# Router and step-size products with stationary weights in four column quarters

## What is computed

```
# each of three expert stages (wg: 1024x4, we: 1024x16)
gl = t @ wg + bg                      # group logits
el = t @ we + be                      # expert logits, 4 groups of 4
... one group, two experts of it per token, their weights; then
... the chosen experts' gate, up and down products
# state-space block (second stack, inside h @ w_in, width 24)
dt    = softplus(dt_raw + dt_bias)    # 16 columns: step sizes
log_f = log_sigmoid(f_raw + forget_b) # 8 columns: forget gates
```

## Time and profile before

| | |
|---|---|
| median of three runs | 1569.85 us (1568.22 to 1571.46) |
| profiled execution | 1570.28 us, span from first to last instruction 1568.5 us |
| mean granted TensorE clock | 0.94 of 2.4 GHz |
| TensorE products busy | 1376.5 us, 88% |
| VectorE, ScalarE, GpSimd busy | 434.8, 238.8, 81.1 us |
| DMA | 357.54 MB, mean 228 GB/s |

### The profile page before, as it was taken

The page is one execution under the profiler, slowest core; times in us unless marked ns, Lnnn a source line. Parts: engine busy times, 40 slices in busy tenths (PEclk is TensorE's granted clock), DMA queues, the critical chain, the costliest instruction groups (busy, mean ns, idle before and its releaser), DMA issues.

```text
span 1568.5 us, 20749 instructions
## 1 busy us (share of the span) xinstructions
PE 1376.5 (88%) x8735; PEld 805.9 (51%) x8735; DVE 434.8 (28%) x1239; ACT 238.8 (15%) x591; POOL 81.1 (5%) x190
## 2 busy tenths in 40 slices
PE   3999889998997788989997999889988899757895
PEld 3446454443445555544446855554555456434574
DVE  1005452222103464432215452421125410001013
ACT  0004210101102353100012121002311120100000
POOL 1110000000010000000001000000000011101010
PEclk9999889999999599899997999899998899998998
DMA  9958627999743365359997333383366389999990
GB/s 324 358 153 293 218 106 267 353 345 324 270 161 109 106 213 165 121 186 365 346 349 255 130 138 108 108 295 107 114 217 206 107 272 333 341 327 294 309 297 28
DMA packets 264103, 357.54 MB, mean 228 GB/s; under 512 B 16086, under 2 KB 184463, under 8 KB 264011
## 3 DMA queue, kind: packets, MB, share of 16 engines
q1 hardware_dynamic: 234082, 335.72, 63.1%
q10 hardware_dynamic: 29929, 20.49, 4.6%
HBM read 355.14 MB, written 1.05 MB: 227 GB/s over the span
## 4 chain that ended last, share of the span: by engine, by line
PE 74%; DMA 12%; DVE 8%; issue 2%; ACT 2%; SPq 1%; POOL 0%; DVEq 0%; ACTq 0%; POOLq 0%
PE bank L1942 18%; PE bank L2104 7%; DMA ring<-in_w_up 5%; PE bank L2130 4%; PE bank L2145 4%; PE bank L2545 4%; PE bank L2162 4%; PE bank L2300 4%; PE bank L2032 4%; DMA ring<-in_w_down 3%; PE bank L1957 3%; PE bank L2592 3%; DMA ring<-in_w_gate 2%; PE bank L2365 2%; PE bank L2270 2%
## 5 line engine op out<-in xcount | busy, mean ns | idle before, releaser
L1942 PE MATMUL bank<-ring,hT 128*128 128x512 f32 x416 | 182.4, 600 | 3.2 <-ACT hT L810 3.0
L1942 PEld LDWEIGHTS bank<-ring,hT 128*128 128x128 f32 x416 | 79.8, 193 | 103.2 <-issue 99.8
L2104 PE MATMUL bank<-ring,A 128*64 128x512 f32 x512 | 113.4, 595 | 6.1 <-issue 3.2
L1942 PE MATMUL bank<-ring,OT 128*128 128x512 f32 x256 | 113.5, 605 | 3.0 <-ACT OT L1096 1.3
L2300 PE MATMUL bank<-ring,A 128*64 128x256 f32 x768 | 94.5, 402 | 23.0 <-DMA ring<-in_w_up 18.0
L1957 PE MATMUL bank<-ring,cact 128*32 128x128 f32 x2304 | 82.4, 297 | 23.2 <-DMA ring<-in_ada_w 14.9
L1957 PEld LDWEIGHTS bank<-ring,cact 128*32 128x32 f32 x2304 | 68.0, 119 | 36.3 <-issue 24.6
L2300 PEld LDWEIGHTS bank<-ring,A 128*64 128x64 f32 x768 | 56.8, 145 | 56.8 <-DMA ring<-in_w_up 20.7
L1942 PEld LDWEIGHTS bank<-ring,OT 128*128 128x128 f32 x256 | 49.4, 194 | 64.7 <-issue 61.0
L2104 PEld LDWEIGHTS bank<-ring,A 128*64 128x64 f32 x512 | 36.2, 137 | 72.0 <-issue 68.7
L2130 PE MATMUL bank<-pb 128*128 128x128 f32 (+1 forms) x512 | 64.4, 279 | 7.7 <-DVE A L1390 5.4
(11 more groups left out here) (405 smaller groups left out, 1651.9 us busy)
## 6 DMA issues: line engine op xcount, KB each, us to landing
ring<-in_ada_w SPq DMA_DIRECT2D x24, 2048.0 KB, 9.0
ring<-in_moe_w_gate SPq DMA_DIRECT2D x32, 1024.0 KB, 7.2
ring<-in_moe_w_up SPq DMA_DIRECT2D x32, 1024.0 KB, 9.9
ring<-in_moe_w_down SPq DMA_DIRECT2D x16, 2048.0 KB, 13.0
ring<-in_w_gate SPq DMA_DIRECT2D x16, 2048.0 KB, 18.5
ring<-in_w_up SPq DMA_DIRECT2D x16, 2048.0 KB, 17.5
ring<-in_w_in SPq DMA_DIRECT2D x13, 2048.0 KB, 12.6
ring<-in_w_mod SPq DMA_DIRECT2D x12, 2048.0 KB, 8.2
```

Of the source, the lines that this page charges most:

```text
L1942: ins = mm(B[2 * (m % 2) + tt][:], lhs[:, c, tt * P:(tt + 1) * P], w[:, c, :], start=c == 0, stop=c == C - 1)
L2104: ins = mm(B[4][n * b:n * (b + 1), :], h3[:, c, n * b:n * (b + 1)], wv[b][:, :, c, :], start=c == 0, stop=c == C - 1)
```

## The change

The roles of the two operands are exchanged. The narrow weights (20 or 24 columns) become stationary, in column quarter q = c mod 4 of the array, and 128 tokens of `hT` move; the result has the logits in the partitions 32q up and the tokens in the free dimension, in `B[2]`, as four partial sums, each of two chunks. A zero product over all partitions starts the bank (`thin_products`). ScalarE copies the 128 x 256 result to SBUF (`thin_copied`, into `PT`), and `thin_folded` multiplies it, as stationary operand, with `fold`, four 24 x 24 identities below one another: this adds the quarters and turns the tokens back into the partitions, in the bank where VectorE expects them. In the three routers the first token tile's products stand ahead of the second tile's transposes; the step sizes' fold stands behind xbc's first tile. `fold` lies in unused columns of `cols`, and GpSimd makes it ahead of the identity. Two waits of VectorE on semaphores of their own (`comb_ready`, `moe_main`) become the general step wait.

```diff
--- before.py
+++ after.py
@@ -249,6 +249,12 @@
         return ap.unsqueeze(axis).broadcast_to(shape)
 
 
+
+
+    fold = cols[:, 320:344]
+    thin = PT[:].rearrange("p a b -> p (a b)")[:, 0:T]
+    THIN = {"h1": 0, "h3": 1, "h4": 2, "h5": 3}
+
     def trans_evacuated(eng, k):
 
         eng.wait_ge(s["tr_act"] if k % 2 == 0 else s["tr_dve"], k // 2 + 1)
@@ -630,7 +636,11 @@
             pool.wait_ge(s["pool_step"], steps[0])
 
         g = nc.gpsimd
+        g.memset(fold, 0.0)
         step(g.memset(ident[:], 0.0))
+        for q in range(4):
+            step(g.affine_select(out=fold, in_=fold, compare_op=ALU.not_equal, fill=1.0, base=-32 * q,
+                                 pattern=[[-1, 24]], channel_multiplier=1))
         step(g.affine_select(out=ident[:], in_=ident[:], compare_op=ALU.not_equal, fill=1.0, base=0,
                              pattern=[[-1, P]], channel_multiplier=1))
         g.memset(zeros[:], 0.0)
@@ -780,6 +790,11 @@
                 if k % 2 == 0:
                     act.wait_ge(s["tr_ready"], k + 1)
                     op(k - TRANS[name], B[4]).then_inc(s["tr_act"], 1)
+
+        def thin_copied(hname):
+
+            act.wait_ge(s["thin_made"], THIN[hname] + 1)
+            a.copy(thin, B[2][:, 0:T]).then_inc(s["thin_out"], 1)
 
         def mod_out(G):
 
@@ -1013,6 +1028,7 @@
         trans_out("h1", modulated(0, 3), [0])
         gate_rows(1)
         trans_out("h1", modulated(0, 3), [1])
+        thin_copied("h1")
         routing_exp(act, "moe0")
         moe_act("moe0")
         mod_out(3)
@@ -1047,10 +1063,12 @@
         act.wait_ge(s["proj_dve"], PROJ_DVE[PROJ["odout"] + 1])
         act.dma_start(rowp[:, 0, :], p["final_g"].partition_broadcast(P)).then_inc(s["rows_param"], 16)
         trans_out("h3", modulated(1, 3), [1])
+        thin_copied("h3")
         routing_exp(act, "moe1")
         moe_act("moe1")
         mod_out(6)
         trans_out("h4", modulated(2, 0))
+        thin_copied("h4")
 
         act.wait_ge(s["dt_abs"], 1)
         a.activation(dts[:, 1], dts[:, 1], ACT.Exp).then_inc(s["dt_exp"], 1)
@@ -1113,6 +1131,7 @@
         trans_out("h5", modulated(2, 3), [0])
         gate_rows(5)
         trans_out("h5", modulated(2, 3), [1])
+        thin_copied("h5")
         act.wait_ge(s["ln_scaled"], 1)
         routing_exp(act, "moe2")
         wide_act()
@@ -1371,9 +1390,8 @@
             step(v.tensor_tensor(rt[:, :, 4, :], rt[:, :, 4, :], rt[:, :, 7, 2:3].broadcast_to([P, TT, 4]), ALU.mult))
             step(v.tensor_tensor(rt[:, :, 5, :], rt[:, :, 5, :], rt[:, :, 7, 3:4].broadcast_to([P, TT, 4]), ALU.mult))
             step(v.tensor_tensor(rt[:, :, 4, :], rt[:, :, 4, :], rt[:, :, 5, :], ALU.add))
-            v.tensor_tensor(comb[:].rearrange("p t (g e) -> p t g e", g=4), bc(rt[:, :, 2, :], 3, [P, TT, 4, 4]),
-                            bc(rt[:, :, 4, :], 2, [P, TT, 4, 4]), ALU.mult).then_inc(s["comb_ready"], 1)
-            dve.wait_ge(s["comb_ready"], i + 1)
+            step(v.tensor_tensor(comb[:].rearrange("p t (g e) -> p t g e", g=4), bc(rt[:, :, 2, :], 3, [P, TT, 4, 4]),
+                                 bc(rt[:, :, 4, :], 2, [P, TT, 4, 4]), ALU.mult))
 
         def experts(name, gate):
             d = MOE[name]
@@ -1443,8 +1461,7 @@
                     step(v.tensor_tensor(tmp[:, h, :], B[2 * tt + h][:], gate[:, 512 * h:512 * (h + 1)], ALU.mult))
                     xs = x[:, tt, 512 * h:512 * (h + 1)]
                     ins = v.tensor_tensor(xs, xs, tmp[:, h, :], ALU.add)
-            ins.then_inc(s["moe_main"], 1)
-            dve.wait_ge(s["moe_main"], i + 1)
+            step(ins)
             moe_rest_dve(name, gate)
 
         def moe_rest_dve(name, gate):
@@ -2052,17 +2069,33 @@
 
             pe.wait_ge(s["max_ready"], max(it["soft"] + 1 for it in items if it["soft"] is not None))
 
-        def router(i, hname):
-
-            if i == 0:
-                pe.wait_ge(s["small_loads"], 16 * NSMALL)
-            for tt in range(TT):
+        def thin_products(w, n, hname, tts=(0, 1)):
+
+            if 0 in tts:
+                mm(B[2][:, 0:T], zeros[:], bc(ident[:], 1, [P, 2, P]), start=True, stop=True)
+            for tt in tts:
                 for g in range(2):
                     trans_evacuated(pe, TRANS[hname] + 2 * tt + g)
                 for c in range(C):
-                    ins = mm(B[7][:, 32 * tt:32 * tt + 20], hT[:, c, tt * P:(tt + 1) * P], wr[i][:, c, :],
-                             start=c == 0, stop=c == C - 1)
-            ins.then_inc(s["router_ready"], 1)
+                    q = c % 4
+                    ins = mm(B[2][32 * q:32 * q + n, tt * P:(tt + 1) * P], w[:, c, 0:n], hT[:, c, tt * P:(tt + 1) * P],
+                             start=False, stop=c >= 4, skip_group_check=True)
+            if 1 in tts:
+                ins.then_inc(s["thin_made"], 1)
+
+        def thin_folded(bank, n, hname):
+
+            pe.wait_ge(s["thin_out"], THIN[hname] + 1)
+            for tt in range(TT):
+                ins = mm(bank[:, 32 * tt:32 * tt + n], thin[:, tt * P:(tt + 1) * P], fold[:, 0:n], start=True, stop=True)
+            return ins
+
+        def router(i, hname):
+
+            if i == 0:
+                pe.wait_ge(s["small_loads"], 16 * NSMALL)
+            thin_products(wr[i], 20, hname, (1,))
+            thin_folded(B[7], 20, hname).then_inc(s["router_ready"], 1)
 
         def places(i):
 
@@ -2459,6 +2492,8 @@
         project("evout", 2, OT)
         token_transposes("h1", xn, "xn_ready", 2, tiles=[0])
         gate_spread(1)
+        pe.wait_ge(s["small_loads"], 16 * NSMALL)
+        thin_products(wr[0], 20, "h1", (0,))
         token_transposes("h1", xn, "xn_ready", 2, tiles=[1])
         pe.wait_ge(s["gate_rows"], 2)
         experts("moe0", "h1")
@@ -2521,6 +2556,7 @@
         project("odout", 2, OT)
         token_transposes("h3", xn, "xn_ready", 6, tiles=[0])
         gate_spread(3)
+        thin_products(wr[1], 20, "h3", (0,))
         token_transposes("h3", xn, "xn_ready", 6, tiles=[1])
         pe.wait_ge(s["gate_rows"], 4)
         experts("moe1", "h3")
@@ -2529,11 +2565,7 @@
         pe.wait_ge(s["moe_added"], 2)
         token_transposes("h4", xn, "xn_ready", 8)
         stage_transposed(pe, "h4")
-        for tt in range(TT):
-            for c in range(C):
-                ins = mm(B[6][:, 32 * tt:32 * tt + 24], hT[:, c, tt * P:(tt + 1) * P], wdf[:, c, :],
-                         start=c == 0, stop=c == C - 1)
-        ins.then_inc(s["dt_ready"], 1)
+        thin_products(wdf, 24, "h4")
 
         for j in range(4):
             m = PROJ["xbc"] + j
@@ -2545,6 +2577,8 @@
                     ins = mm(B[2 * (m % 2) + a // 2][:, (a % 2) * T:(a % 2 + 1) * T], w[:, c, a * P:(a + 1) * P],
                              hT[:, c, :], start=c == 0, stop=c == C - 1)
             ins.then_inc(tile_used, 1)
+            if j == 0:
+                thin_folded(B[6], 24, "h4").then_inc(s["dt_ready"], 1)
 
         pe.wait_ge(s["a_ready"], 1)
         for tt in range(TT):
@@ -2640,6 +2674,7 @@
         project("wo", 2, OT)
         token_transposes("h5", xn, "xn_ready", 10, tiles=[0])
         gate_spread(5)
+        thin_products(wr[2], 20, "h5", (0,))
         token_transposes("h5", xn, "xn_ready", 10, tiles=[1])
         pe.wait_ge(s["gate_rows"], 6)
         wide_experts()
```

More of the change, by code:

```diff
@@ L2053, in attention @@
             pe.wait_ge(s["max_ready"], max(it["soft"] + 1 for it in items if it["soft"] is not None))
+        def thin_products(w, n, hname, tts=(0, 1)):
+            if 0 in tts:
+                mm(B[2][:, 0:T], zeros[:], bc(ident[:], 1, [P, 2, P]), start=True, stop=True)
+            for tt in tts:
+                for g in range(2):
+                    trans_evacuated(pe, TRANS[hname] + 2 * tt + g)
+                for c in range(C):
+                    q = c % 4
[8 more added lines that the diff above has]
+            return ins
         def router(i, hname):
@@ L2058, in router @@
                 pe.wait_ge(s["small_loads"], 16 * NSMALL)
-            for tt in range(TT):
-                for g in range(2):
-                    trans_evacuated(pe, TRANS[hname] + 2 * tt + g)
-                for c in range(C):
-                    ins = mm(B[7][:, 32 * tt:32 * tt + 20], hT[:, c, tt * P:(tt + 1) * P], wr[i][:, c, :],
-                             start=c == 0, stop=c == C - 1)
-            ins.then_inc(s["router_ready"], 1)
+            thin_products(wr[i], 20, hname, (1,))
+            thin_folded(B[7], 20, hname).then_inc(s["router_ready"], 1)
         def places(i):
```

## The result

The changed kernel took 1546.49 us (median of 4 runs, 1542.55 to 1547.86), the kernel before 1569.03 us beside it (4 runs, 1565.24 to 1571.46): ratio 0.9854, 95% interval 0.9827 to 0.9882. The profiled execution took 1542.55 us, span 1540.7, so it is the fastest of its four: 3.9 us under the median.

The account below looks back on a forecast made before the run. TensorE was taken to bound the kernel, with 74% of the chain of waits. Gains of 2.3 + 2.3 + 1.5 + 3.7 = 9.8 us gave a forecast of 1560.1 us, range 1556.8 to 1565.

Parts of the forecast that it names:

- What bounds: TensorE holds 74% of the chain of waits, and all four products to be changed stand on that path.
- The quarter product's price: Each quarter instruction on TensorE costs 57 ns at half clock and 30 ns at full, as at line 1957.
- rival A: Quarters overlap less than at line 1957, up to 226 ns each: 1580 us at worst, about 1573 at full clock; 5%.
- ScalarE's copy and the hand-overs: Between quarter products and fold, ScalarE's copy takes 0.37 us, with two hand-overs 0.5 us.
- First and second router: Routers of the first two expert stages, zero products behind keeping their pace: 2.3 us gained at each.
- Third router: Third expert stage, without zero products: routing starts 1.1 us sooner at half clock, 2.0 at full; 1.5 taken.
- Step sizes: Ahead of xbc: xbc starts 4.2 us sooner, less 0.5 for the fold, 3.7 us net; bounds 0 and 4.5.
- At nothing: GpSimd's added setup, an estimated 1.8 us, stays covered before TensorE's first instruction; merged VectorE waits also cost nothing.
- Does it reach the end: The gain passes through the DMA-bound last stage, because the load queue stood 120.6 us waiting for TensorE to free slices.
- Rival B: Filled gap keeps TensorE at 2.4 GHz into the zero products, choice ends last: 12.9 us gained, 1557 us; 15%.
- C: Hand-overs cost more, or VectorE's dt steps delay the convolution until TensorE waits: 1564 us; 13%.
- D: DMA holds the end: the last stage streams at its own pace, the shift is lost, about 1568 to 1570; 5%.

Follow-up runs that it names:

- the two halves: Changed kernel with only the routers in the new form (1559.38 us, 0.9921 of the kernel before), and with only the step sizes (1562.87 us, 0.9948).
- the late-tile run: Changed kernel with each router's first-tile quarter products moved behind the second tile's transposes: 1556.75 us, ratio 0.9903 to the kernel before.
- the third stage's filler: Changed kernel plus four zero products of 512 columns behind the third stage's fold: 1551.32 us; with six more around the step sizes' transposes, 1543.37 us.

## Why the prediction was wrong

In the order of its steps:

- **What bounds.** Right. All four products stood on the path; each edit alone gave time, and the two halves multiply to the whole.
- **The quarter product's price.** Right. 57 and 30 ns were taken; it measured 0.63 us for 16 with the tail (1.00) and 1.92 us for 32 (0.50), 60 ns each. Each of them lasts 273 or 421 ns, so they overlap, and rival A is out. The rule cited for it, that loads overlap products in flight only in another row group (the Trainium skill, "TensorE: Matmul & The Clock Gate", Part 3), doesn't hold for column quarters in any of these traces: 16 loads of 99 ns, 1.6 us end to end, passed with their products in the same 0.63 us. Nor does that page of the Trainium skill speak against the change as a whole, as the prediction has it: the same Part gives a measured speedup of 2.38 for three products side by side in column tiles, with 32 stationary and 512 moving columns each.
- **ScalarE's copy and the hand-overs.** Right: the copy took 0.37 us, and from the quarters' end to the fold it was 0.48 us where 0.5 were taken. The fold was given 1.06 us at half clock, 0.8 at full; it took 0.62 to 0.63 in the three routers, at full clock.
- **First and second router.** This is where it failed, with two steps. The first is the clock behind the product. "These start at 218.0 and, as now, low at first", and "keep their length": the clock after the router was taken from the profile of before, where the old product had kept it down. In the second stage the windows went from 0.50 and 0.59 to 1.00 and 1.00; zero products 3.68 us in place of 6.23. The other step is the upper bound. It counted how much sooner VectorE starts, and forgot that with the choice last the place products gain their old lateness too (0.8 and 1.6 us). By the prediction's own numbers 225.67 - 221.9 = 3.8 us for the first, not 3.1 (and its lower bound 225.67 - 218.0 - 6.9 = 0.8, not 1.0). Measured, against 2.3 and 2.3: in the first 3.5 us, or 5.0 in the profile where 1.1 of them are evout's projection, and 5.4 us in the second. There the second tile's transposes ran at full clock too, 1.09 us in place of 1.97.
- **Third router.** 2.1 us against 1.5: the right mechanism, just past its end for the full clock (2.0), and the clock was full.
- **Step sizes.** Ahead of xbc 3.84 us against 4.2 taken, with 1.19 us for the zero product and not 0.86. But all of it is 5.6, not 3.7. "it begins at half clock, in both kernels" was false for the changed one: the first tile of xbc stood at 0.85 before and at 0.99 after, 16.3 against 14.17 us. With the fold in xbc's way for 0.4 us (856.88 to 857.25) the sum is 3.84 + 2.13 - 0.37 = 5.6. VectorE's delay reached nobody, as forecast.
- **At nothing.** Right: GpSimd's last mark moved from 5.04 to 6.49, TensorE's first instruction stands at 7.00, on the same DMA.
- **Does it reach the end.** The totals agree with that: they gained about as much as the stretches ahead of the last stage (below). But a scatter of 12 us in that stage (245.6 to 257.2) hides any term of 2 us.
- **Rival B** had the right effect and the wrong cause. It was given 15% because the filled gap would keep the clock; the late-tile run leaves that gap open and has the clock back for the zero products all the same. Filling the gap is worth 0.2 to 0.9 us a stage. B's own time, 1557, was also 10 us too long. C did not come, and of D only the scatter.
- **What no step had**: 3.4 us in the state-space stage, where no line changed. It is time at half clock that went (17.1 us of it before, 10.2 after; worked out in the last section), so the prediction's mistake is the same, the old clock kept for the changed kernel; how the change reaches so far is not shown. The second expert stage, between its first gather and h4, kept its length (173.6 us in all five profiles).

The four places gave 16.6 to 18.2 us for 9.8 forecast; with the 3.4 us, 20.0 to 21.6; the three comparisons gave 22.9, 20.9 and 21.8 us (the median of before times one less the ratio), with intervals 4 to 7 us to either side. So the gain is accounted for within what was measured; whether a further microsecond or two is the change's stays open. The last stage's 9.2 us of the first pair were luck: the two later profiles of the changed kernel have nothing of them. And why the clock fell or came back at each place, no run shows.

## What to carry to other kernels

A thin product on TensorE has two prices: its own time, and the clock at which everything directly behind it runs; read the granted clock of the windows after it as well as its own, and don't keep the old clock for them once the product is changed. Bound a gain where the next waiter stands (here the place products), not where the first one does. Where runs of one kernel scatter by more than the term in question, compare stretches between fixed marks in several traces of the same code.

## What was not expected of the hardware

**The clock has phases.** Same code, same stretch, another clock. The windows of z's projection to its output, seventh and eighth of 15 us, in the kernel before and after:
```profile
1002.72:1017.72 15.00, 10.08 (x41) 8.24 (x39) 8.11 (x18) 1.26 (x2) 0.00 (x0) 0.59 0.33 126
1017.72:1032.72 15.00, 12.20 (x277) 11.01 (x277) 10.31 (x25) 1.81 (x6) 2.45 (x2) 0.84 0.68 242
```
```profile
989.92:1004.92 15.00, 9.45 (x57) 7.81 (x59) 8.82 (x20) 1.26 (x2) 0.00 (x0) 0.73 0.33 125
1004.92:1019.92 15.00, 12.13 (x272) 10.34 (x262) 10.73 (x28) 2.87 (x9) 2.45 (x2) 0.93 0.78 282
```
The six windows ahead of them agree to 0.01 us in the work of TensorE and all stand at 1.00. A window of 15 us at 0.59 has 2 x 0.41 x 15 = 12.3 us at half clock; so before it is 12.3 + 4.8 = 17.1 us in the two windows, and after it is 8.1 + 2.1 = 10.2 us. Half of the 6.9 us between them is the 3.4 us that this stretch gave. No edit is near, and the seven variants of the kernel took 116.9 to 120.0 us there. The stretch from od_in's projection to od_out's took 215.9 to 216.0 us in five profiles, 213.1 in one and 208.6 to 210.1 in six, with both forms among the short ones (the old one only widened) and among the long ones; the zero products of the first stage took 5.37, 5.38 and 3.68 us in three profiles of one code; the third stage's filler 3.68 and 6.63. The second stage, 43.5 us in three profiles of the changed kernel, took 43.95 in three variants that leave it as it is. What sets the phase was not tried.

**The last stage's DMA.** From 1310 to 1430 us, where the engines are full throughout, the core's DMA moved 315 to 331 GB/s in all twelve profiles, and the stretch from the second pass's transposes to the end took from 245.6 to 263.9 us in twelve, with no order by kernel: 245.6, 254.7 and 257.2 for the changed one.

**Column quarters.** 32 instructions in quarters, with 128 moving columns, 8.7 us laid end to end at 273 ns and 13.5 at 421, passed in 1.07 us at full and 1.92 at half clock. 32 full-width ones took 3.73 us at full clock with 120 moving columns, and 6.86 us at half clock with 20.
